# Half of the modulation projection moved into the attention phase, on GpSimd

## The reference

```python
m_lat = silu(c) @ w_mod + b_mod            # w_mod is 1024 x 6144, float32
m_ctx = silu(c_ctx) @ w_mod + b_mod
sh1, sc1, g1, sh2, sc2, g2 = split(m_lat, 6)
sh1c, sc1c, g1c, sh2c, sc2c, g2c = split(m_ctx, 6)
h = modulate(x, sh1, sc1)                  # and ctx with sh1c, sc1c
y = token_mixer(h, h_ctx, ...)             # recurrence and windowed attention, @ w_out
x = layer_norm(ALPHA * x + g1 * y, ...)
h = modulate(x, sh2, sc2)
y = hier_moe(h, ...)                       # routed experts
x = layer_norm(ALPHA * x + g2 * y, ...)
```

## Time and profile before

| | us |
|---|---|
| median of 3 runs (lowest, highest) | 2148.46 (2146.95, 2149.47) |
| the profiled execution's own time | 2146.1 |
| its span in the trace | 2144.2 |
| TensorE busy | 1797.0 (84%) |
| VectorE busy | 1498.0 (70%) |
| ScalarE busy | 1038.7 (48%) |
| GpSimd busy | 425.3 (20%) |

### The profile page before, as it was taken

One profiled execution on the slowest core, in us unless ns is written; L12 is line 12 of the kernel. 1 busy time (PEld: TensorE's weight loads), 2 busy tenths in 40 slices (PEclk: granted clock), 3 DMA queues, 4 the chain that ended last, 5 costly groups with the idle time before them and its releaser, 6 DMA issues. The chain is left out here.

```text
span 2144.2 us, 41310 instructions
## 1 busy us (share of the span) xinstructions
PE 1797.0 (84%) x11738; PEld 1025.2 (48%) x11741; DVE 1498.0 (70%) x1859; ACT 1038.7 (48%) x1360; POOL 425.3 (20%) x407
## 2 busy tenths in 40 slices
PE   2388888898769997999923999999999898899947
PEld 0066666533357776555512444545444444444422
DVE  1357676478879998788978335766769898665537
ACT  1144434387658887333203224445547667544326
POOL 0000000000012222333312111223323333222113
PEclk7789999999979998999955999999999999999979
DMA  9812121267451112244326447886979999887637
GB/s 367 312 60 99 54 93 40 109 200 258 170 201 59 59 59 81 99 157 147 137 75 245 144 113 248 293 269 217 363 231 381 371 373 372 300 276 212 196 79 274
DMA packets 167723, 417.64 MB, mean 195 GB/s; under 512 B 16160, under 2 KB 24768, under 8 KB 163952
## 3 DMA queue, kind: packets, MB, share of 16 engines
q1 hardware_dynamic: 152832, 362.87, 46.3%
q0 software_dynamic: 14832, 54.01, 10.3%
HBM read 343.39 MB, written 73.45 MB: 194 GB/s over the span
## 5 line engine op out<-in xcount | busy, mean ns | idle before, releaser
L1988 DVE SCALAR_TENSOR_TENSOR arena<-arena 128x2048 f32 (+1 forms) x186 | 420.7, 2288 | 107.9 <-ACT arena L1932 51.4
L2068 PE MATMUL ps<-arena 128*128 x1200 | 459.9, 383 | 42.2 <-DVE arena L1988 42.0
L2069 PE MATMUL ps<-arena 128*128 x1200 | 459.6, 383 | 0.0
L2070 PE MATMUL ps<-arena 128*128 x1200 | 458.8, 382 | 0.0
L1926 ACT ACTIVATE arena<-arena 128x2048 f32 (+1 forms) x124 | 233.2, 1908 | 150.6 <-DMA arena<-w 63.3
L619 PE MATMUL ps<-arena 128*128 128x256 f16 (+1 forms) x1680 | 234.9, 301 | 21.1 <-DVE arena L504 21.1
L2068 PEld LDWEIGHTS ps<-arena 128*128 128x128 f16 x1200 | 118.3, 99 | 183.2 <-issue 57.6
L619 PEld LDWEIGHTS ps<-arena 128*128 128x128 f16 x1680 | 164.6, 99 | 85.6 <-DVE arena L504 15.2
L2070 PEld LDWEIGHTS ps<-arena 128*128 128x128 f16 x1200 | 118.5, 99 | 141.8 <-issue 5.2
L2069 PEld LDWEIGHTS ps<-arena 128*128 128x128 f16 x1200 | 118.2, 98 | 132.1 <-issue 4.3
L1932 ACT ACTIVATE arena<-arena 128x2048 f32 (+1 forms) x62 | 117.2, 1907 | 66.2 <-DMA arena<-w 47.9
(11 more groups left out here) (289 smaller groups left out, 3155.6 us busy)
## 6 DMA issues: line engine op xcount, KB each, us to landing
arena<-w SPq DMA_DIRECT2D x186, 1024.0 KB, 12.7
arena<-hT_d SPq DMA_DIRECT2D x64, 512.0 KB, 5.9
arena<-w_mod SPq DMA_DIRECT2D x12, 2048.0 KB, 18.2
h_d<-arena SPq DMA_DIRECT2D x17, 512.0 KB, 3.0
x_d<-arena SPq DMA_DIRECT2D x17, 512.0 KB, 2.6
arena<-x SPq DMA_DIRECT2D x8, 1024.0 KB, 6.2
hT_d<-arena SPq DMA_DIRECT2D x16, 512.0 KB, 3.7
arena<-x SPq DMA_DIRECT2D x16, 512.0 KB, 4.7
```

Source lines behind the costliest of these rows:

```text
L1988: return nc.vector.scalar_tensor_tensor(dst, src, scale, high, ALU.mult, ALU.subtract)
L2068: pe.matmul(out, high, part(buf, whi, at, 512), start=first, stop=False)
L2069: pe.matmul(out, high, part(buf, wlo, at, 512), start=False, stop=False)
L2070: return pe.matmul(out, low, part(buf, whi, at, 512), start=False, stop=last)
```

## The change

The front phase makes only the first three rows (sh1, sc1, g1: 3072 of the 6144 columns), in 8 slabs 1536 columns wide instead of 12 of 2048. VectorE's two groups of low parts keep their places, now behind the first and the second half. The other three rows (sh2, sc2, g2) are made in the attention phase, for the latent stream alone: SP loads eight slabs of 128 x 3072 (1.5 MB each: the row block k of w_mod), two up front and one after each of the first six pairs. GpSimd multiplies slab k in place by the column silu(c)[k] (a per-partition scalar, kept in `c_col`) and adds it to a running sum `late`, in three pieces of 1024 columns: two behind `inverse(i, 0)` and one behind `inverse(i, 1)`, and the g1 multiplication is moved behind that. Row 0 of `late` starts as b_mod, all others as zero. At the start of the output phase TensorE adds `late` over the 128 partitions with eight products with a matrix of ones, ScalarE copies the result out of PSUM, SP stores it to `mod_rows`, and loads sh2 and sc2 from there. The loops of SP and GpSimd over the pairs are written out.

```diff
-    RING, WIDE = 4, 2048
-    THIRDS = 6 * D // WIDE
+    RING, WIDE = 4, 1536
+    NARROW = WIDE // 4
+    HALVES = FRONT // WIDE
...
+            nc.scalar.activation(g["c_col"][:], c2s.rearrange("p (k s) -> p s k", s=2)[:, 0], ACT.Silu)
...
             dve.wait_ge(c_ld, 80)
-            for i in range(THIRDS):
+            for i in range(HALVES):
                 dve.wait_ge(mod_mm, RING * (i + 1))
...
-                for k in range(4 * i, 4 * i + 4) if i < 2 else ():
+                for k in range(4 * i, 4 * i + 4):
...
-            for name, src in (("g1", g["mod_rows"][0:1, 2 * D:3 * D]), ("sh2", g["mod_rows"][0:1, 3 * D:4 * D]),
-                              ("sc2", g["mod_rows"][0:1, 4 * D:5 * D]), ("l1g", g["ln1"][0:1, :]),
+            for name, src in (("g1", g["mod_rows"][0:1, 2 * D:3 * D]), ("l1g", g["ln1"][0:1, :]),
...
+            sp.wait_ge(late_ok, LATE_OK + 1)
+            sp.dma_start(late[0:1, :], g["b_mod"][0:1, FRONT:6 * D]).then_inc(late_ok, 16)
+
+            def load_late(k):
+                if k > 1:
+                    sp.wait_ge(late_d, LATE_D + 2 * LATE_P * (k - 1))
+                sp.dma_start(slab[k % 2], g["w_mod"][k * P:(k + 1) * P, FRONT:6 * D]).then_inc(late_ld[k % 2], 16)
...
+                if i + 2 < KD:
+                    load_late(i + 2)
...
+            nc.gpsimd.memset(late, 0.0).then_inc(late_ok, 1)
+
+            def late_terms(k, lo, hi):
+                if lo == 0:
+                    pool.wait_ge(late_ld[k % 2], LATE_LD + 16 * (k // 2) + 16)
+                    pool.wait_ge(late_ok, LATE_OK + 17)
+                for n in range(lo, hi):
+                    at = LATE_D + 2 * (LATE_P * k + n)
+                    cols = slice(n * D, (n + 1) * D)
+                    nc.gpsimd.tensor_scalar(slab[k % 2][:, cols], slab[k % 2][:, cols], g["c_col"][:, k:k + 1], None, ALU.mult)                        .then_inc(late_d, 1)
+                    pool.wait_ge(late_d, at + 1)
+                    nc.gpsimd.tensor_tensor(late[:, cols], late[:, cols], slab[k % 2][:, cols], ALU.add).then_inc(late_d, 1)
+            for i in range(PAIRS):
                 inverse(i, 0)
...
+                late_terms(i, 0, 2)
+                inverse(i, 1)
+                late_terms(i, 2, LATE_P)
+
+                pool.wait_ge(w_ld, START + 16 * 7)
+                row = arena[:, OUT_W0 + i * D:OUT_W0 + (i + 1) * D]
                 nc.gpsimd.tensor_tensor(row, row, ow["g1"], ALU.mult).then_inc(w_gate, 1)
-                inverse(i, 1)
...
+            rows_d = g["mod_rows"][0:1, FRONT:6 * D].rearrange("s (i m n) -> m s i n", i=2, m=4)
+            sp.wait_ge(late_ev, LATE_EV + 1)
+            for m in range(4):
+                sp.dma_start(rows_d[m], late_rows[32 * m:32 * m + 1]).then_inc(late_st, 16)
+            sp.wait_ge(late_st, LATE_ST + 64)
+            for name, at in (("sh2", 3 * D), ("sc2", 4 * D)):
+                sp.dma_start(b[name], g["mod_rows"][0:1, at:at + D].to_broadcast([P, D])).then_inc(late_ld, 16)
...
             def first():
-                nc.vector.tensor_scalar(b["sc2"], b["sc2"], 1.0, None, ALU.add).then_inc(w_ok, 1)
                 for k in range(C_RNN):
...
+                    dve.wait_ge(late_ld, LATE_LD + 32)
+                    nc.vector.tensor_scalar(b["sc2"], b["sc2"], 1.0, None, ALU.add).then_inc(w_ok, 1)
+                    dve.wait_ge(w_ok, START + 1)
...
             def first():
+                act.wait_ge(late_mm, LATE_MM + 1)
+                nc.scalar.activation(late_rows, ps[:, 0:2, 0:LATE_N], ACT.Copy).then_inc(late_ev, 1)
                 for k in range(C_RNN):
                     high_w(k)
...
             def first():
                 pe.wait_ge(p_ok, START + 2)
+                for i in range(2):
+                    for m in range(4):
+                        mm = pe.matmul(ps[32 * m:32 * m + 32, i, 0:LATE_N], b["ones"],
+                                       late[:, (4 * i + m) * LATE_N:(4 * i + m + 1) * LATE_N], start=True, stop=True)
+                mm.then_inc(late_mm, 1)
                 transposes_a(0, 0)
                 column_sums(0)
```

More of the change, by code:

```diff
@@ L198, in phase_modulation @@
     mod_mm, rows_done, rows_st = sem("a_mod_mm"), sem("a_rows_done"), sem("a_rows_st")
-    a = arena_slices(arena, 0, [(f"w{j}", 2 * WIDE) for j in range(RING)] + [("rows", THIRDS * 512), ("spare", D)])
+    a = arena_slices(arena, 0, [(f"w{j}", 2 * WIDE) for j in range(RING)] + [("rows", HALVES * NARROW), ("spare", D)])
     ring = [a[f"w{j}"].rearrange("p (k n) -> p k n", k=2) for j in range(RING)]
-    rows = [a["rows"][32 * m:32 * m + 2, :].rearrange("p (i n) -> p i n", i=THIRDS) for m in range(4)]
+    rows = [a["rows"][32 * m:32 * m + 2, :].rearrange("p (i n) -> p i n", i=HALVES) for m in range(4)]
     c2s = small[:, 0:2 * KD]
@@ L222, in _ @@
                 sp.dma_start(raw[:, :, dst:dst + size], w_in[:, :, src:src + size]).then_inc(win_ld, 16)
-            for n in range(RING, RING * THIRDS):
+            for n in range(RING, RING * HALVES):
                 sp.wait_ge(mod_mm, n - RING + 1)
@@ L916, in phase_attention @@
     w_ld, w_gate, s_edge = sem("d_w_ld"), sem("d_w_gate"), sem("b_idh")
+    late_ld, late_ok, late_d = g["done"]["wmod_ld"][0:2], g["done"]["wmod_ld"][3], g["done"]["win_hi"]
+    LATE_LD, LATE_OK, LATE_D = DONE["wmod_ld"], DONE["wmod_ld"], DONE["win_hi"]
+    late = late_modulation(arena)
+    slab = [arena[:, LATE_W * (j + 1):LATE_W * (j + 2)] for j in range(2)]
+    assert 3 * LATE_W <= KT0
+    LATE_P = LATE_W // D
     ow = output_weights(arena)
@@ L980, in _ @@
                 .then_inc(w_ld, 16)
+            sp.wait_ge(late_ok, LATE_OK + 1)
[4 more added lines that the diff above has]
+                sp.dma_start(slab[k % 2], g["w_mod"][k * P:(k + 1) * P, FRONT:6 * D]).then_inc(late_ld[k % 2], 16)
+            for k in range(2):
+                load_late(k)
             def store(i, j):
@@ L986, in store @@
                 sp.dma_start(g["attn_d"][bass.ds(t, 1)].rearrange("n p d -> (n p) d"), b[f"o{j}"]).then_inc(o_st[j], 16)
-            with sp.Fori(0, PAIRS - 1) as i:
+            for i in range(PAIRS - 1):
                 for j in range(2):
@@ L1483, in column_sums @@
                     pe.wait_ge(lg, START + t - 3)
-                pe.matmul(ps[:, 7, 64:65], b["ysum"], b["ones"], start=True, stop=True).then_inc(ssm, 1)
+                pe.matmul(ps[:, 7, 64:65], b["ysum"], b["ones"][:, 0:1], start=True, stop=True).then_inc(ssm, 1)
             def product(t, j, k):
```

34 lines of the change are left out of this document (23 added, 11 removed).

## The result

| | before | changed |
|---|---|---|
| median, us (runs) | 2148.97 (4) | 2131.6 (4) |
| lowest to highest | 2146.95 to 2150.58 | 2130.82 to 2131.96 |
| span of the profiled execution | 2144.2 | 2129.0 |

The ratio is 0.9926, with a 95% interval of 0.9912 to 0.9940: the change makes the kernel faster by 0.7%, 16 us. The prediction was 2130.3 us.

A forecast was written before the change was run, and what follows sets the result against it. Transfers bound the first phase; VectorE and ScalarE set attention's pace. On the profiled execution 2146.1 - 26.4 + 1.5 + 2.9 + 3.8 = 2127.9 us, 18.2 less, so a median of 2130.3 us; range 2122 to 2140.

The forecast's parts named there:

- First phase: Front phase: half the bytes removed, VectorE's second low parts become its end; second phase starts at 69.4 us, gain 26.4 us.
- One sign that I had named as wrong: First phase: slabs landing more than 3.9 us apart would show the forecast wrong.
- The price of the multiplication: GpSimd in attention: multiplying 1024 columns by a per-partition column takes 1.6 us, range 1.0 to 2.4.
- a sign of being wrong: GpSimd in attention: L1069, the multiplication by a column, lasting above 2.8 us.
- Steady state: Attention tiles: GpSimd's inverse and two pieces take 12.9 us, under the tile's 13.85, so nothing is lost.
- ScalarE's slack: Attention tiles: GpSimd may be about 1.5 us late at each tile before ScalarE stands still.
- First pair: Attention's first tile pair: slab 0 lands late, so ScalarE stands 1.5 us; delayed queries overlap; range 0 to 4.
- End: Attention's end: one piece, the g1 product and L1081 follow the last inverse unhidden; 2.9 us lost, range 2.3 to 3.7.
- Output phase: Output phase's start: ones, eight products and ScalarE's copy delay its chain 3.8 us, range 2.4 to 5; sc2's reload hidden.
- the rivals: GpSimd becomes the bound, 0.05; GpSimd a little late, 0.08; output entry hides, 0.12; front phase gives less, 0.07.
- a GpSimd that is a little late each tile: Attention: at 3.3 us for the multiplication, 9.2 us more, time 2139 to 2140 us; chance 0.08.

The follow-up runs named there:

- experiment 2: The changed kernel with all eight groups of VectorE's low parts ahead of the second half's additions; 2125.44 us, ratio 0.9905 to the kernel before.
- experiment 5: The changed kernel with three MEMSETs and eight priced GpSimd instructions more at the start of the first phase; executed once, 2128.15 us.
- Experiment 8: The changed kernel with GpSimd's 24 multiplications by a column written as two-input products with the column broadcast; 2129.22 us, ratio 0.9919 to the kernel before.
- experiment 3: The changed kernel with the second late slab's load issued behind the first refill of masks and queries; 2130.72 us, ratio 0.9927 to the kernel before.
- Experiment 6: The changed kernel with GpSimd's pieces and g1 products spread over the gaps behind the first fifteen inverses, slab loads moved to match; 2125.75 us, ratio 0.9915.
- Experiment 4: The changed kernel with ScalarE's copy of the late rows behind its first four high parts; 2127.28 us, ratio 0.9916 to the kernel before.

## Why the prediction was right, step by step

**First phase, 26.4 us forecast, 26.9 measured.** That VectorE's splits would end it was right, and experiment 2 shows it. The last slab came at 55.31, 1.3 us sooner than worked out. The product was at the dear end of its bounds (2.74, where I took 2.0 within 1.4 to 2.7), and the barrier took 0.26 us and not the 0.5 that I gave it. One sign that I had named as wrong did come: the last slab's product starts 4.79 us after the one before it, more than 3.9, but the 1.3 us in hand hold that already.

**The price of the multiplication, 1.6 us forecast within 1.0 to 2.4, 2.85 measured.** This step failed. I took the two-input addition for the upper end, since one input seemed no dearer than two, and drew a slope through two small instructions of different lines. The form itself is slower than the addition (experiment 5). The Trainium skill, "GPSIMD Engine Reference", section 4.1, has one-input operations at roughly line rate: the copy comes near it (1.04 us for 1024 columns), the TENSOR_SCALAR, at 2.80, does not, and the measurement decides. 2.85 us is also above the 2.8 that I had named as a sign of being wrong, and just above the 2.83 from which I had ScalarE wait in each tile.

**Steady state, nothing forecast, +0.2 measured from the third to the fifteenth inverse.** The time was right, the picture only in part. I had expected L1045 right behind the tile's last minimum in all but the first pair, and in the second tile of every pair GpSimd comes late: some 14.6 us from the first inverse of a pair to the second, where it was 14.3 before. Two things kept that inside ScalarE's slack. A piece with a multiplication of 2.85 us takes 5.26 us, and not the 5.52 that my 0.15 us for each of its two waits would make it. And my 13.85 us was the last tile; the other second tiles are those 14.3 us long, and the mean from the second inverse to the sixteenth is 201.75 / 14 = 14.41. So 0.3 us of ScalarE's 1.5 are used up in most pairs, 0.8 in the last, and it waits for GpSimd in the first pair alone. That is luck in part: the price lay outside my range, and a wait priced too high and a tile taken too short made up for it. Experiment 8, whose cheaper form won nothing there, shows that GpSimd's list was not waited for.

**First pair, 1.5 us forecast, 3.3 measured at the third inverse** (50.73 us into the phase, 47.45 before). The mechanism was right: slab 0 at 27.1 us into the phase as forecast, then a late inverse. The size follows from the price: two pieces of 5.3 instead of 4.3 us are 1.9 us more. By the same sum the second inverse would be 3.1 + 1.9 = 5.0 us late, of which ScalarE's slack takes 1.5; it was 4.9. The late queries, which I had overlapping, did overlap (experiment 3).

**End, 2.9 forecast, 3.6 measured behind the fifteenth inverse.** The dearer piece costs 0.9 us more than I had, the barrier 0.2 less. The first table shows only 2.7 for this stage, because the last inverse began 0.8 us later than its tile's end allowed and then waited less for ScalarE: 3.57 us from its start to its end, where 4.34 stood. Experiment 6 takes this term away.

**Output phase, 3.8 forecast, 3.75 measured at the column sum, 4.9 over the whole phase.** The chain was right to 0.1 us: the products 2.79, the copy 0.81 (2.7 and 0.85 forecast). Experiment 4 shows that ScalarE's place in it was the cost. The other 1.1 us build up behind: 0.3 by the second tile, then some 0.05 a tile to the end, in every kernel that has the change. In ten tiles from the middle of the phase ScalarE's first squares wait 7.3 us for their attention tile from DRAM where they waited 4.7 before the change, and TensorE's transposes 1.6 us for VectorE instead of 1.0. No run here tests why.

Over all, by the second cut, the errors are +1.8 us in the first pair, +0.2 in the steady state, +0.7 at the end of attention and +1.1 in the output phase, against -0.5 in the first phase and -0.2 in the next: +3.0 together. 15.2 us were gained between the two profiled spans where 18.2 were forecast, and 17.4 between the medians. So 2.5 of the 3 us come from one wrong price, and the median's 1.3 us from the forecast is closer than the working deserved. None of the rivals came about as a time; the one of a GpSimd that is a little late each tile came about in kind, in the second tile of every pair, but within ScalarE's slack, and the price at which it would have cost something was all but reached.

## What to carry to other kernels

When a transfer-bound phase loses half its bytes, ask what stood in the transfers' shadow: here 8 us of splits became the new end, and moving them repaired 5.6 us, as much as any other edit. Work handed to an engine that is idle on average costs what it adds where that engine's list is waited for: here in the first tiles, whose data is late, and behind the last one, where nothing hides it; spread it over the gaps in between and leave the last gap empty (5.4 us of the attention phase here). Lateness read at an instruction of the late engine itself is not yet time lost: cut the phase at instructions that waited for somebody else. And a price that no row shows should be measured by itself or bounded from above by more than a neighbour that merely looks dearer.

## What the runs showed of the hardware

On GpSimd, for 128 x 1024 float32, a multiplication by a scalar (constant or per-partition column) took 2.77 to 2.86 us, the two-input addition 2.34 to 2.37, the two-input product with a broadcast column 1.89, a copy 1.04 and a MEMSET 0.95. So the two-input form with the column broadcast is a third cheaper than the one-input form that looks made for it.
